# Prompt attention by token parity, in units of 512 columns, two heads issued in alternation

## The chip, the cores and the metric

The kernel runs on one core of a Trainium2 chip. Times are device microseconds of one execution. Five engines work beside each other: TensorE (PE, with its weight loads as PEld), VectorE (DVE), ScalarE (ACT), GpSimd (POOL) and SyncE (SP, which issues most DMAs). TensorE's clock is granted at one of two levels, 1.2 or 2.4 GHz, shown as 0.5 and 1.0 of full speed.

## The reference

One inference step of a two-layer decoder, for a prompt of 256 tokens and 32 sample tokens (8 sequences of 4) together, in float32. Each layer: RMSNorm, one input projection to pool, query, key, value and gate columns, a pooling branch, an attention branch, a merge, and a feed-forward part (dense in layer 0, top 2 of 8 experts in layer 1). What the change touches is the attention of the prompt:

```
ATT_GROUPS = ((128, 1), (512, 4), (2048, 16))     # window, dilation of 3 head groups, 8 heads of 64 each
sc = einsum('bnqhd,bnkhd->bnhqk', qs, kb) * 64 ** -0.5 - slope * distance    # keys at 0 <= distance <= window,
                                                                              # distance a multiple of the dilation
o, lse = softmax(sc) @ v, logsumexp(sc)
y = sum over the 3 groups of o * softmax over the groups of lse
```

For one head number and one query, mixing the three groups by their denominators is one softmax over the keys of all three groups side by side. In the groups with dilation 4 and 16 a query at an even token sees keys at even tokens alone, and one at an odd token keys at odd tokens. The normalised keys and the values of the prompt are outputs too.

## The kernel before

The whole program is written out per engine, each with its own instruction order; PSUM's eight banks are handed out ahead of time by `plan` (one list of jobs per section, in which each name takes the next bank of its pool). `wait_free` waits for a bank, `wait_full` for its data, `wait_read` until it has been read.

A layer's attention part begins with 40 column tiles of the input projection (four pool tiles and n = 0 to 35), each of 24 float32r matmuls over 288 tokens. Queries and keys stand transposed in `qT` and `kT` (dimension on partitions, two heads of 64 per tile). Behind certain column tiles follow the jobs of `AFTER` (line 178). `ROW_TILES` (line 182) puts the jobs "kt" and "vt" there: keys and values of a group are turned to token rows, keys copied by DVE to one of two `k_tok` buffers and stored by POOL's DMAs, values copied by ACT to `v_tok`. DVE waits for the store of two row tiles ago before it overwrites a buffer.

Then comes the prompt attention: 16 units per layer (line 140), one for each pair of heads `j` (0 to 3), tile of 128 queries `qt` and head `e` of the pair. With `qt` = 0 a unit has 3 x 128 score columns, with `qt` = 1 it has 3 x 256. For a unit,

- `scores` (line 889, PE) multiplies 128 queries with the keys, one matmul for each group (float32, two records each in the trace), contracting over the 64 partitions of the head;
- DVE adds the distance table times the slope (line 1652) and takes the maximum (1659), ACT the exponential with its sum (1336), DVE the reciprocal (1662), POOL scales the probabilities in place (2007);
- `turn_probs` (902, PE) turns the probabilities in tiles of 128, ACT copies them to `probsT`;
- `values` (913, PE) multiplies with `v_tok`, into 64 partitions of a bank that both heads share; DVE copies it to `attT`.

The loop at line 1000 issues in step u: scores of unit u, turns of unit u - 2, values of unit u - 3, and from u = 3 on two cache tiles. A cache tile (`cache_step`, 987) belongs to the sample tokens' attention: a 128 x 512 piece of the key cache is turned by four PE instructions and copied by ACT (even tiles) or DVE (odd ones). Four tiles make a chunk of 1 MB, which is then scored by 16 matmuls of 32 query columns (`score_chunk`, 960); one slot of the five-slot ring is free for SP's next DMA as soon as its chunk is turned. `score_new` (949), the scores of the sample's own keys, stands behind tile 2. 32 of the 72 tiles of keys are done within the loop, the others behind it, then the cache's values, the merge and the output projection.

POOL's order before the first `scale`: the stores of all row tiles, then, once the last value tile is read, a memset of 5632 columns for the sample's query tiles, then the scales, with `place_queries` behind each of the first two.

Of the kernel before, what the change touches and what calls it, by code (L numbers as in the profile page):

```python
# [69 lines left out]
def shape_constants():  # L70
# [4 lines left out]
    dist = np.full((PART, G, 2, PART), MASKED)  # L75
    for g in range(G):
        for kind in range(2):
            d = p - f + PART * (1 - kind)
            ok = (d >= 0) & (d <= SPAN[g]) & (d % DIL[g] == 0)
            dist[:, g, kind] = np.where(ok, d, MASKED)  # L80
# [82 lines left out]
FIRST_UNIT = 3  # L163


def unit_tiles(u):
    at = 2 * (u - FIRST_UNIT)
    return [m for m in (at, at + 1) if 0 <= m < NT]


REST = unit_tiles(len(UNITS) + 2)[-1] + 1

# [26 lines left out]
def section_attention():  # L199
# [7 lines left out]
    for u in range(len(UNITS) + 3):  # L207
        if u < len(UNITS):
            js += [(("S", u, n), UPOOL) for n in range(1 + UNITS[u][1])]
        if 2 <= u < len(UNITS) + 2:  # L210
            js += [(("T", u - 2, n), UPOOL) for n in range(1 + UNITS[u - 2][1])]
        if u >= 3 and UNITS[u - 3][2] == 0:
            js.append((("O", UNITS[u - 3][0], UNITS[u - 3][1]), UPOOL))
        js += [(("kT", 0, m), UKPOOL) for m in unit_tiles(u)]
# [107 lines left out]
def build(nc, io):  # L322
# [9 lines left out]
    with ctx:  # L332
# [51 lines left out]
        dist = view(take(G * 2 * 128), G, 2 * 128)  # L384
# [36 lines left out]
        probs = [view(p_at + 768 * i, 768) for i in range(3)]  # L421
        probsT = [view(p_at + 768 * (3 + i), 768) for i in range(2)]
# [121 lines left out]
        p_ready = Tally(sem("probs_ready"), 16)  # L544
# [210 lines left out]
        def _(e):  # L755
# [56 lines left out]
            def attention(L):  # L812
# [33 lines left out]
                def turn_rows(job, tile, a, n, count=4):  # L846

                    S.wait_free(e, job)
                    for i in range(count):
                        turn(S.ps(job)[0:n, 128 * i:128 * (i + 1)], tile(i)[:, a:a + n],  # L850
                             full[S.bank(job)] if i == count - 1 else None)

# [3 lines left out]
                for n in range(36):  # L856
# [3 lines left out]
                    for job in AFTER.get(n, []):  # L860
# [28 lines left out]
                def scores(u):  # L889
                    j, qt, he = UNITS[u]  # L890
                    p = slice(64 * he, 64 * he + 64)
                    w = 128 * (qt + 1)
                    for n in range(1 + qt):
                        S.wait_free(e, ("S", u, n))
                    for g in range(G):
                        job = ("S", u, 1 if qt and g == 2 else 0)
                        last = g == 2 or (qt and g == 1)
                        at = 0 if qt and g == 2 else g * w
                        mm(S.ps(job)[:, at:at + w], qT[p, 4 * g + j, 128 * qt:128 * qt + 128],
                           kT[p, 4 * g + j, 0:w], True, True, full[S.bank(job)] if last else None)  # L900

                def turn_probs(u):
                    j, qt, he = UNITS[u]
                    e.wait_ge(p_ready.sem, p_ready.at(L, u + 1))
                    n = G * (qt + 1)
                    for i in range(n):
                        job = ("T", u, i // 4)
                        if i % 4 == 0:
                            S.wait_free(e, job)
                        turn(S.ps(job)[:, 128 * (i % 4):128 * (i % 4 + 1)], probs[u % 3][:, 128 * i:128 * (i + 1)],  # L910
                             full[S.bank(job)] if i == n - 1 or i % 4 == 3 else None)

                def values(u):
                    j, qt, he = UNITS[u]
                    job = ("O", j, qt)
                    if he == 0:
                        S.wait_free(e, job)
                    for n in range(1 + qt):
                        S.wait_read(e, ("T", u, n))
                    n = G * (qt + 1)  # L920
                    for i in range(n):
                        g, kt = i // (qt + 1), i % (qt + 1)
                        h = 2 * j + he
                        mm(S.ps(job)[64 * he:64 * he + 64, 0:128], v_tok[:, kt, g, 64 * h:64 * h + 64],
                           probsT[u % 2][:, 128 * i:128 * (i + 1)], i == 0, i == n - 1,
                           full[S.bank(job)] if he == 1 and i == n - 1 else None)
# [71 lines left out]
                S.wait_read(e, ("kt", 2, 2))  # L998
                S.wait_read(e, ("vt", 2, 2))
                for u in range(len(UNITS) + 3):  # L1000
                    if u < len(UNITS):
                        scores(u)
                    if 2 <= u < len(UNITS) + 2:
                        turn_probs(u - 2)
                    if u >= 3:
                        values(u - 3)
                    for m in unit_tiles(u):
# [230 lines left out]
        def _(e):  # L1238
# [46 lines left out]
            def attention(L):  # L1285
# [6 lines left out]

                split_high(L, 2)
                for n in range(37):
# [32 lines left out]
                for u in range(len(UNITS) + 3):  # L1327
                    if 2 <= u < len(UNITS) + 2:
                        v = u - 2
                        for n in range(1 + UNITS[v][1]):  # L1330
                            w = min(512, 128 * G * (UNITS[v][1] + 1) - 512 * n)
                            copy(S, ("T", v, n), probsT[v % 2][:, 512 * n:512 * n + w], S.ps(("T", v, n))[:, 0:w])
                    if u < len(UNITS):
                        w = 128 * G * (UNITS[u][1] + 1)
                        e.wait_ge(max_ready.sem, max_ready.at(L, u + 1))
                        e.activation(probs[u % 3][:, 0:w], probs[u % 3][:, 0:w], ACT.Exp, bias=stats[:, u:u + 1],
                                     accum_out=stats[:, 16 + u:17 + u]).then_inc(exp_ready.sem, 1)
                    for m in unit_tiles(u):
                        cache_copy(m)
# [770 lines left out]
```

## Time and profile before

| | |
|---|---|
| median of 3 runs | 2279.5 us (2277.4 to 2279.97) |
| profiled execution | 2273.52 us, span 2271.6 us |
| mean granted clock of TensorE | 0.954 |
| TensorE busy | 2125.1 us (94%) |
| VectorE busy | 1397.4 us (62%) |
| ScalarE busy | 1148.7 us (51%) |
| GpSimd busy | 162.5 us (7%) |
| read from HBM | 542.15 MB, 242 GB/s over the span |

Busy shares are means over stages with different limits, so a stage has to be looked at by itself. Matmuls are pipelined and their ends are modelled: a group of them is shown a little longer than the distance to the next group's start. The prompt attention lies near 185 to 268 us for layer 0 and near 874 to 956 us for layer 1.

### The profile page before, as it was taken

The page shows a single profiled execution, that of the slowest core. Times are in us where ns is not written, and L with a number is a line of the kernel's source. Part 1 is how long each engine was busy: PE and PEld are TensorE (multiplying, and loading weights), DVE is VectorE, ACT ScalarE, POOL GpSimd, SP SyncE. Part 2 cuts the span into 40 slices and gives each one's busy share as a digit, 9 for nine tenths or more (in the row PEclk, how much of TensorE's full clock was granted, in tenths as well). Part 3 has the DMA queues.
Part 4 walks back from the last instruction along what each step waited for, and adds up shares of the span by engine and source line. Part 5 has one row for each costly group of instructions (what it writes and reads, how often), then busy time and mean ns, then how long its engine had stood idle before and what let it go on. Part 6 is the DMA issues. An engine that isn't in the chain of part 4 may idle for free.

```text
span 2271.6 us, 33081 instructions
## 1 busy us (share of the span) xinstructions
PE 2125.1 (94%) x13193; PEld 1801.2 (79%) x13194; DVE 1397.4 (62%) x1338; ACT 1148.7 (51%) x1107; POOL 162.5 (7%) x244
## 2 busy tenths in 40 slices
PE   6998986989999998987988999999999999999998
PEld 6987744989998987753987787887878787887876
DVE  4454422444435444421437888888898888888886
ACT  3443322334433433421325766667676667667674
POOL 0113100102210113200100000000000000000000
PEclk9998987989999998986998999999999999999999
DMA  7442488435544442469427999999999999999994
GB/s 225 155 139 96 131 306 269 154 112 163 166 167 146 159 137 93 149 217 321 149 75 251 352 339 332 352 322 349 331 338 335 343 350 317 356 323 345 335 338 173
DMA packets 292914, 551.19 MB, mean 243 GB/s; under 512 B 10708, under 2 KB 107132, under 8 KB 292658
## 3 DMA queue, kind: packets, MB, share of 16 engines
q1 hardware_dynamic: 288592, 541.53, 68.4%
q0 software_dynamic: 3072, 8.00, 1.0%
q8 instruction: 84, 1.38, 0.2%
q10 hardware_dynamic: 1138, 0.06, 0.0%
q14 instruction: 28, 0.23, 0.0%
HBM read 542.15 MB, written 7.76 MB: 242 GB/s over the span
## 4 chain that ended last, share of the span: by engine, by line
PE 79%; DVE 10%; issue 5%; DMA 3%; ACT 1%; POOL 1%; DVEq 0%; SPq 0%; ACTq 0%; POOLq 0%
PE psum L766 73%; PE psum L774 6%; DVE expert_split L1849 5%; DMA low_part<-in_cache_kv_g 2%; DMA low_part<-in_w_in 1%; DVE low_part L1902 1%; ACT w_split L1261 1%; DVE w_split L1514 1%; POOL high_part L2002 0%; DVE high_part L1525 0%; DVE high_part L1521 0%; DMA high_part<-in_const_a 0%; DVE low_part L1915 0%; DVE hT_split L1855 0%; POOL merged_split L2058 0%
## 5 line engine op out<-in xcount | busy, mean ns | idle before, releaser
L1849 DVE TENSOR_TENSOR expert_split<-low_part,expert_split 128x2048 fp32r<-128x2048 f32 x336 | 764.2, 2288 | 91.2 <-ACT expert_split L1448 91.2
L1448 ACT ACTIVATE expert_split<-low_part 128x2048 fp32r<-128x2048 f32 x336 | 644.1, 1918 | 204.0 <-PE psum L766 202.1
L766 PE MATMUL psum<-expert_split,xe_split 128*128 128x512 f32 x2688 | 638.9, 394 | 11.3 <-DVE expert_split L1849 10.2
L766 PEld LDWEIGHTS psum<-expert_split,xe_split 128*128 128x128 f32 x2688 | 496.9, 188 | 136.4 <-DVE expert_split L1849 27.8
L766 PE MATMUL psum<-xn_split,w_split 128*128 128x288 f32 x3744 | 520.4, 300 | 26.0 <-DVE xn_split L1529 14.4
L766 PEld LDWEIGHTS psum<-xn_split,w_split 128*128 128x128 f32 x3744 | 509.8, 191 | 40.7 <-issue 24.5
L1514 DVE TENSOR_TENSOR w_split<-low_part,w_split 128x2048 fp32r<-128x2048 f32 x105 | 240.9, 2295 | 366.5 <-ACT w_split L1261 366.5
L1261 ACT ACTIVATE w_split<-low_part 128x2048 fp32r<-128x2048 f32 x105 | 200.9, 1913 | 375.1 <-PE psum L766 275.4
L766 PE MATMUL psum<-expert_split,hT_split 128*128 128x512 f32 x1344 | 319.1, 397 | 0.0
L766 PEld LDWEIGHTS psum<-expert_split,hT_split 128*128 128x128 f32 x1344 | 250.8, 188 | 58.7 <-DVE expert_split L1849 2.1
L766 PE MATMUL psum<-low_part 128*128 128x128 f32 (+5 forms) x1198 | 211.8, 449 | 35.5 <-DMA low_part<-in_cache_kv_g 25.1
L766 PEld LDWEIGHTS psum<-low_part 128*128 128x128 f32 (+3 forms) x1198 | 130.5, 173 | 103.2 <-DMA low_part<-in_cache_kv_g 46.4
L774 PE MATMUL psum<-high_part,low_part 128*128 128x128 f32 (+2 forms) x1097 | 159.4, 288 | 23.1 <-DMA high_part<-in_const_a 9.6
L1507 DVE COPY low_part<-psum 128x512 f32<-128x512 f32 (+7 forms) x110 | 64.2, 590 | 173.4 <-PE psum L774 114.4
L774 PEld LDWEIGHTS psum<-high_part,low_part 128*128 128x128 f32 (+2 forms) x1097 | 128.9, 146 | 53.0 <-issue 20.8
L1241 ACT ACTIVATE low_part<-psum 128x512 f32<-128x512 f32 (+2 forms) x144 | 77.1, 557 | 158.1 <-PE psum L774 151.0
L1915 DVE TENSOR_TENSOR low_part<-low_part,psum 128x512 f32<-128x512 f32 x56 | 38.5, 688 | 54.0 <-PE psum L766 54.0
L766 PE MATMUL psum<-hid_split,w_split 128*128 128x288 f32 x528 | 70.1, 294 | 0.0
L766 PEld LDWEIGHTS psum<-hid_split,w_split 128*128 128x128 f32 x528 | 70.0, 188 | 0.0
L766 PE MATMUL psum<-low_part,high_part 128*32 128x128 f32 (+1 forms) x1260 | 59.5, 289 | 8.7 <-POOL high_part L2020 4.9
L766 PE MATMUL psum<-branch_split,w_split 128*128 128x288 f32 x384 | 55.8, 306 | 10.1 <-DVE branch_split L1727 10.1
L766 PE MATMUL psum<-merged_split,w_split 128*128 128x288 f32 x384 | 56.7, 313 | 7.6 <-POOL merged_split L2058 7.6
(134 smaller groups left out, 1065.5 us busy)
## 6 DMA issues: line engine op xcount, KB each, us to landing
low_part<-in_we_gate SPq DMA_DIRECT2D x112, 1024.0 KB, 5.2
low_part<-in_we_up SPq DMA_DIRECT2D x112, 1024.0 KB, 6.4
low_part<-in_we_down SPq DMA_DIRECT2D x112, 1024.0 KB, 6.1
low_part<-in_cache_kv_g SPq DMA_DIRECT2D x72, 1024.0 KB, 5.5
low_part<-in_w_in SPq DMA_DIRECT2D x56, 1024.0 KB, 5.1
low_part<-in_w_dense SPq DMA_DIRECT2D x33, 1024.0 KB, 5.3
low_part<-in_w_out SPq DMA_DIRECT2D x8, 1024.0 KB, 4.9
low_part<-in_w_branch_pool SPq DMA_DIRECT2D x8, 512.0 KB, 5.4
```

What stands on the lines that cost most here:

```text
L766: signal(e.matmul(out, lhsT, rhs, start=start, stop=stop, skip_group_check=mixed), inc)
L774: signal(e.transpose(out, in_, ident[0:in_.shape[0], 0:in_.shape[0]]), inc)
L1241: S.freed(e.activation(out, in_, ACT.Copy), job)
L1261: e.activation(w_split[gw % SRING][:, 0, :], view(slot(c), CH), ACT.Copy).then_inc(hi_ready, 1)
L1448: e.activation(e_split[v % MSRING][:, 0, :], view(slot(v, MRING), CH), ACT.Copy).then_inc(hi_ready, 1)
L1507: S.freed(e.tensor_copy(out, in_), job)
L1514: e.tensor_tensor(s[:, 1, :], view(slot(c), CH), s[:, 0, :].bitcast(F32), ALU.subtract).then_inc(lo_ready, 1)
L1849: e.tensor_tensor(w[:, 1, :], view(slot(v, MRING), CH), w[:, 0, :].bitcast(F32), ALU.subtract)\
L1902: I.freed(e.tensor_tensor(x, x, I.ps(job)[0:n], ALU.add), job)
L1915: I.freed(e.tensor_tensor(m_h[c % 2], m_sig[c % 2], I.ps(("eu", c)), ALU.mult), ("eu", c))
```

## The change

Units are now (j, qt), with `qt` the parity of the query tokens (even or odd), and a unit has 512 score columns: 256 keys of group 0 and the 128 keys of the same parity of groups 1 and 2. The two heads of a unit are issued in alternation, scores and values alike, each with its own PSUM bank for scores and turned probabilities. The order of a step, the order of the scales and the place of the first scores are new. Value rows of groups 1 and 2 lie sorted by parity in `v_tok` (and are stored to every second row of the output), the output of a unit goes to every second token of `attT`.

```diff
-    return [(j, qt, e) for j in range(J) for qt in range(2) for e in range(2)]
+    return [(j, qt) for j in range(J) for qt in range(2)]
+NU = len(UNITS)
+BLOCK_AT, BLOCK_W = (0, 256, 384), (256, 128, 128)
+ACT_SCALED = 2
+def step_tiles(v, part):
+    at = BH * (v - FIRST_STEP) + 2 * part          # FIRST_STEP = 2
+    return [m for m in (at, at + 1) if 0 <= m < NT]
+REST = step_tiles(NU, 1)[-1] + 1
+SCORES_AT = 34
...
+        if n == SCORES_AT:
+            js += [(("S", 0, he), SUMS) for he in range(2)]
+    for v in range(NU + 1):
+        if v + 1 < NU:
+            js += [(("S", v + 1, he), UPOOL) for he in range(2)]
+        js += [(("kT", 0, m), UKPOOL) for m in step_tiles(v, 0)]
+        if v >= 1:
+            js.append((("O", v - 1), UPOOL))
+        js += [(("kT", 0, m), UKPOOL) for m in step_tiles(v, 1)]
+        if v < NU:
+            js += [(("T", v, he), UPOOL) for he in range(2)]
...
-        probs = [view(p_at + 768 * i, 768) for i in range(3)]
+        probs = [view(p_at + 512 * i, 512) for i in range(4)]
...
+        def tile_tokens(row, qt):
+            return row.rearrange("p (a r) -> p r a", r=2)[:, qt, :]
... TensorE
+                def scores(v):
+                    j, qt = UNITS[v]
+                    for he in range(2):
+                        S.wait_free(e, ("S", v, he))
+                    for g in range(G):
+                        at, w = BLOCK_AT[g], BLOCK_W[g]
+                        for he in range(2):
+                            p = slice(64 * he, 64 * he + 64)
+                            keys = kT[p, 4 * g + j, 0:SEQ]
+                            mm(S.ps(("S", v, he))[:, at:at + w], tile_tokens(qT[p, 4 * g + j, 0:SEQ], qt),
+                               tile_tokens(keys, qt) if g else keys, True, True,
+                               full[S.bank(("S", v, he))] if g == G - 1 else None)
-                            turn_rows(job, lambda k: vT[i][:, k, :], *TT[job[2]])
+                            turn_rows(job, lambda k: vT[i][:, k, :], *TT[job[2]], strided=i > 0 and job[2] < 2)
+                    if n == SCORES_AT:
+                        S.wait_read(e, ("bc", 23))
+                        scores(0)
+                def turn_probs(v):         # per head: wait for its scale (p_first or p_ready), four turns
+                def values(v):
+                    for i, (g, kt) in enumerate(((0, 0), (0, 1), (1, qt), (2, qt))):
+                        for he in range(2):
+                            h = 2 * j + he
+                            mm(S.ps(job)[64 * he:64 * he + 64, 0:128], v_tok[:, kt, g, 64 * h:64 * h + 64],
+                               probsT[he][:, 128 * i:128 * (i + 1)], i == 0, i == 3,
+                               full[S.bank(job)] if (he, i) == (1, 3) else None)
-                S.wait_read(e, ("kt", 2, 2))
-                S.wait_read(e, ("vt", 2, 2))
+                for v in range(NU + 1):
+                    if v + 1 < NU:
+                        scores(v + 1)
+                    for m in step_tiles(v, 0):
+                        cache_step(m)
+                    if v == 1:
+                        S.wait_read(e, ("vt", 2, 2))
+                    if v >= 1:
+                        values(v - 1)
+                    for m in step_tiles(v, 1):
+                        cache_step(m)
+                    if v < NU:
+                        turn_probs(v)
... ScalarE (soften: wait for the maximum, Exp of 512 columns; scale: wait for the reciprocal, Copy with scale)
+                        if c == 35:
+                            soften(0)
+                            soften(1)
+                scale(0)
+                scale(1)
+                for v in range(NU + 1):
+                    for he in range(2):
+                        for m in step_tiles(v, he):
+                            cache_copy(m)
+                        if v + 1 < NU:
+                            soften(2 * (v + 1) + he)
+                    if v < NU:
+                        for he in range(2):
+                            copy(S, ("T", v, he), probsT[he], S.ps(("T", v, he)))
+                    if v + 1 < ACT_SCALED:
+                        for he in range(2):
+                            scale(2 * (v + 1) + he)
... VectorE (biased: three scalar_tensor_tensor and the maximum of a unit; inverted: its reciprocal)
+                    if c == SCORES_AT + 1:
+                        inverted(0)
+                        inverted(1)
+                    if c == SCORES_AT:             # behind the row copies of this c
+                        biased(0)
+                        biased(1)
+                for v in range(NU + 1):
+                    for he in range(2):
+                        if v + 1 < NU:
+                            biased(2 * (v + 1) + he)
+                        if he == 1 and v + 1 < NU:
+                            inverted(2 * (v + 1))
+                        for m in step_tiles(v, he):
+                            cache_copy(m)
+                    if v + 1 < NU:
+                        inverted(2 * (v + 1) + 1)
+                    if v >= 1:
+                        j, qt = UNITS[v - 1]
+                        copy(S, ("O", v - 1), tile_tokens(attT[:, j, 0:SEQ], qt), S.ps(("O", v - 1))[:, 0:128])
... GpSimd
+                e.wait_ge(zeroed.sem, zeroed.at(L, 1))
+                for he in range(2):
+                    place_queries(0, he)
+                for u in range(2 * ACT_SCALED, 2 * NU):
+                    scale(u)
```

## Rows read from the trace of the kernel before

**Rows 1.** The page's busy table: busy us, share of the span, instructions.

```profile
PE 2125.1 (94%) x13193; PEld 1801.2 (79%) x13194; DVE 1397.4 (62%) x1338; ACT 1148.7 (51%) x1107; POOL 162.5 (7%) x244
```

**Rows 2.** Windows by stage: stretch, its length, busy per engine, granted clock, DMA share.

```profile
185.00:195.00 10.00, 5.28 (x24) 3.77 (x25) 4.76 (x15) 2.78 (x7) 9.17 (x15) 0.56 0.26 93
206.00:214.00 8.00, 8.00 (x43) 6.78 (x46) 2.00 (x6) 1.97 (x5) 0.58 (x1) 0.57 0.42 133
214.00:250.00 36.00, 36.00 (x361) 28.89 (x364) 20.45 (x53) 16.29 (x37) 5.97 (x8) 1.00 0.35 114
```

**Rows 3.** Chain of waits, 140 to 350 us: start, length, what the chain ran through.

```profile
182.32 2.29 DMA out_kv_prompt<-high_part
...
187.70 4.80 POOL high_part L2002
...
249.80 2.50 PE psum L766 x38
...
322.47 10.87 DMA low_part<-in_cache_kv_g
```

**Rows 4.** TensorE's timeline, one period: start, length, line, operation, count.

```profile
231.84 1.08 PE L766 MATMUL psum<-low_part,high_part 128*32 128x128 f32 x32
232.85 1.56 PE L766 MATMUL psum<-low_part 64*128 64x256 f32 x6
234.34 0.55 PE L774 MATMUL psum<-high_part,low_part 128*128 128x128 f32 x3
234.82 1.52 PE L766 MATMUL psum<-low_part 128*64 128x128 f32 x12
236.27 1.09 PE L774 MATMUL psum<-high_part,low_part 128*128 128x128 f32 x8
...
242.09 0.93 PE L766 MATMUL psum<-low_part 64*128 64x128 f32 x6
242.96 0.88 PE L774 MATMUL psum<-high_part,low_part 128*128 128x128 f32 x6
243.76 0.87 PE L766 MATMUL psum<-low_part 128*64 128x128 f32 x6
...
249.73 1.08 PE L766 MATMUL psum<-low_part,high_part 128*32 128x128 f32 x32
```

**Rows 5.** TensorE's timeline at the stage's start and end.

```profile
185.36 3.40 PE L766 MATMUL psum<-low_part 64*128 64x128 f32 x18 [1.95 <-DVE high_part L1507]
193.12 0.90 PE L774 MATMUL psum<-high_part,low_part 128*128 128x128 f32 x3 [4.36 <-POOL low_part L2007]
...
199.11 1.47 PE L774 MATMUL psum<-high_part,low_part 128*128 128x128 f32 x8
...
203.47 2.76 PE L766 MATMUL psum<-low_part,high_part 128*128 128x32 f32 x24
...
264.73 1.09 PE L774 MATMUL psum<-high_part,low_part 128*128 128x128 f32 x8
...
266.76 1.52 PE L766 MATMUL psum<-low_part 128*64 128x128 f32 x12
```

**Rows 6.** TensorE's timeline: four matmuls on the whole array, four on row strips.

```profile
110.22 0.77 PE L766 MATMUL psum<-high_part,low_part 32*128 32x288 f32 x8
...
142.32 2.10 PE L766 MATMUL psum<-low_part 128*128 128x288 f32 x8
```

**Rows 7.** Groups by line and shape, 185 to 272 us, and ScalarE's, 214 to 259 us.

```profile
L1652 DVE SCALAR_TENSOR_TENSOR low_part<-high_part,psum 128x256 f32<-128x256 f32 x24 | 8.7, 416 | 10.2 <-PE psum L766 10.1
L1659 DVE TENSOR_REDUCE high_part<-low_part 128x1 f32<-128x768 f32 x8 | 7.6, 953 | 0.8
L1652 DVE SCALAR_TENSOR_TENSOR low_part<-high_part,psum 128x128 f32<-128x128 f32 x24 | 5.5, 282 | 4.4 <-PE psum L766 4.2
L1659 DVE TENSOR_REDUCE high_part<-low_part 128x1 f32<-128x384 f32 x8 | 4.4, 553 | 0.3
...
L1336 ACT ACTIVATE low_part<-low_part,high_part 128x768 f32<-128x768 f32 x6 | 5.6, 939 | 4.6 <-DVE high_part L1659 4.6
```

**Rows 8.** VectorE's timeline: the third key row copies of groups 1 and 2.

```profile
180.15 0.68 DVE L1507 COPY high_part<-psum 32x512 f32<-32x512 f32 x1 [2.01 <-DMA out_kv_prompt<-high_part]
...
184.63 0.68 DVE L1507 COPY high_part<-psum 32x512 f32<-32x512 f32 x1 [0.92 <-DMA out_kv_prompt<-high_part]
```

More of the change, by code:

```diff
@@ L74, in shape_constants @@
     band = (np.arange(2 * QUAD)[None, :] == QUAD + p // HD)
[L75 to L80, printed above, removed]
+    dist = np.zeros((PART, 6 * PART))
+    keys = np.arange(SEQ)[None, :]
+    for at, g, d in ((0, 0, 2 * p - keys), (SEQ, 0, 2 * p + 1 - keys), (2 * SEQ, 1, 2 * (p - f)), (2 * SEQ + PART, 2, 2 * (p - f))):
+        ok = (d >= 0) & (d <= SPAN[g]) & (d % DIL[g] == 0)
+        dist[:, at:at + d.shape[1]] = np.where(ok, d, MASKED)
     inv = np.zeros((PART, PG, 16))
@@ L383, in build @@
         band = view(take(2 * QUAD), 2 * QUAD)
-        dist = view(take(G * 2 * 128), G, 2 * 128)
+        dist = view(take(6 * 128), 6 * 128)
         inv_count = view(take(PG * 16), PG, 16)
@@ L885, in attention @@
                             S.wait_read(e, ("zv", 4 * i + 3))
-                            turn_rows(job, lambda k: vT[i][:, k, :], *TT[job[2]])
[L889 to L911, printed above, removed]
@@ new lines, in attention @@
+                    if n == SCORES_AT:
[3 more added lines that the diff above has]
+                    for he in range(2):
+                        job, u = ("T", v, he), 2 * v + he
+                        if v < ACT_SCALED:
+                            e.wait_ge(p_first.sem, p_first.at(L, u + 1))
+                        else:
+                            e.wait_ge(p_ready.sem, p_ready.at(L, u + 1 - 2 * ACT_SCALED))
+                        S.wait_free(e, job)
+                        for i in range(4):
+                            turn(S.ps(job)[:, 128 * i:128 * (i + 1)], probs[u % 4][:, 128 * i:128 * (i + 1)],
+                                 full[S.bank(job)] if i == 3 else None)
@@ L1592, in mean, with biased, inverted @@
                         .then_inc(mean_ready.sem, 1)
+                def biased(u):
+                    v, he = u // 2, u % 2
+                    j, qt = UNITS[v]
+                    job, p = ("S", v, he), probs[u % 4]
+                    S.wait_full(e, job)
+                    for g in range(G):
+                        at, w = BLOCK_AT[g], BLOCK_W[g]
+                        table = SEQ * qt if g == 0 else 2 * SEQ + PART * (g - 1)
+                        r = e.scalar_tensor_tensor(out=p[:, at:at + w], in0=dist[:, table:table + w],
+                                                   scalar=-float(SLOPES[g, 2 * j + he]), in1=S.ps(job)[:, at:at + w],
+                                                   op0=ALU.mult, op1=ALU.add)
+                    S.freed(r, job)
+                    S.wait_read(e, job)
+                    e.tensor_reduce(stats[:, u:u + 1], p, AX.X, ALU.max, negate=True).then_inc(max_ready.sem, 1)
+                def inverted(u):
+                    e.wait_ge(exp_ready.sem, exp_ready.at(L, u + 1))
+                    e.reciprocal(stats[:, 32 + u:33 + u], stats[:, 16 + u:17 + u]).then_inc(rden_ready.sem, 1)
                 rows = 0
@@ new lines, in attention @@
+                for v in range(NU + 1):
+                    for he in range(2):
+                        if v + 1 < NU:
[8 more added lines that the diff above has]
+                        j, qt = UNITS[v - 1]
+                        copy(S, ("O", v - 1), tile_tokens(attT[:, j, 0:SEQ], qt),
+                             S.ps(("O", v - 1))[:, 0:128])
```

110 lines of the change are left out of this document (24 added, 86 removed).

## The prediction, on record before the result

> **What bounds the kernel now.** I read the page's busy table first, then windows by stage, then the chain of waits, then TensorE's timeline through one period of the prompt attention. TensorE is busy for 94% of the span [rows 1], but that average hides stages. The change touches one stage of each layer: from the last column tile of the input projection to the last prompt unit, about 183 to 268 us in layer 0 [rows 5, 8], and the same stretch of layer 1, where shapes and order are the same; I work layer 0 and count it twice.
>
> The stage has two halves. At 185 to 195 TensorE is busy for 5.28 of 10 us at a mean clock of 0.56: a start-up in which it waits. From 214 to 250 it is busy for 36.00 of 36 us at clock 1.00, while VectorE has 20.45 and the DMA share is 0.35 [rows 2]. The chain says the same: a 4.80 us GpSimd memset in the start-up, then matmul groups with no wait between them [rows 3]. So the steady part is paid in TensorE time, and TensorE time saved there is saved on the clock, as long as no other engine is late.
>
> One period (four units, eight cache tiles, two score chunks) runs from 231.84 to 249.73, 17.89 us [rows 4]. Each group's busy time overlaps the next by 0.07 us; less that, scores take 1.49 (two key tiles) and 0.86 (one), turns of probabilities 0.48 and 0.81, values 1.45 and 0.80, a pair of cache tiles 1.02, a chunk 1.01. Two of each unit kind, four tile pairs, two chunks: 2 x 5.89 + 4.08 + 2.02 = 17.88, so the period is accounted for. Two units cost 5.89 us on average.
>
> **The change, part by part.** *Fewer columns.* Two old units of the two kinds (averaged) stream 1152 score columns, 9 turns and 9 value matmuls; a new pair (both heads of one parity) streams 1024, 8 and 8. Eight pairs per layer either way. By the widths above a new pair one after the other would cost: scores 2 x 0.50 + 4 x 0.29 = 2.16, turns 1.04, values 8 x 0.242 = 1.94, together 5.14. That alone saves 0.75 per pair.
>
> *Halves side by side.* The heads alternate instruction by instruction; scores contract over partitions 0-63 and 64-127 into different PSUM banks, values write partitions 0-63 and 64-127. The trace shows no 64-wide pair in alternation, but the 32-wide case: four 288-column matmuls on four row strips take 0.77 us where four on the whole array take 2.10 [rows 6], 2.7 times faster; sixteen 128x128 matmuls on column strips take 1.01, 0.063 each against 0.242 for the 64-wide ones in a row [rows 4]. So strips do overlap. Bounds for a scores pair: 2.16 (no overlap) to 1.08 (full); for values 1.94 to 0.97. I take 1.1 and 1.0, near the full end because both strip rows are. A pair then costs 1.1 + 1.04 + 1.0 = 3.14, saving 2.75.
>
> Against this speaks the Trainium skill, "TensorE: Matmul & The Clock Gate", Part 3: it measured 3.07 for four row tiles, not 4. That agrees with the 2.7 here; if two tiles lost in the same proportion (a factor near 1.5, my estimate from that page), scores plus values would be 2.7 instead of 2.1 and the total gain 10 us smaller, inside my range.
>
> *Strided operands.* Queries, the keys of two groups and sixteen turned value tiles are now read at every second token. No row shows a strided TensorE operand; nearest are the contiguous ones. Below: nothing. Above, if a strided stream took twice as long: 0.58 per pair (two of three score waves) and 16 turns at 0.13, together 6.7 us per layer. I take nothing; the upper end goes into the range. The stores of value rows go to alternate rows of the output, rows as long as before, and only the end of the layer waits for them: nothing.
>
> *The start.* Removed: the memset ahead of the first scale (ScalarE now scales the first four units), and 1.95 us of waiting before the first scores [rows 5]. Added: VectorE does bias and maximum of units 0 and 1 among its last row copies, and waits for ScalarE's exponentials before the copies of group 2. VectorE's third copy for group 1 ends at 180.83 whatever is changed, as it waits for a store [rows 8]. One new unit of 512 columns: 0.42 + 2 x 0.28 + 0.69 for the maximum (between 0.55 at 384 and 0.95 at 768 columns) = 1.67 [rows 7]. Two units end at 184.2, the second exponential (0.8, from 0.94 at 768 columns) at 185.0; two row copies at 0.68 to 186.4; the third needs the first one's store to land (2.29 in the chain, [rows 3], after its issue of 0.5), and ends near 189.2. It frees a PSUM bank that the first turn of probabilities needs, and behind it on VectorE stand the biases of units 2 and 3, which ScalarE waits for. What goes with the memset comes back as this queue. From there TensorE goes at half clock, as in the windows and in a turn of three at 0.90 instead of 0.55 [rows 5]: turn 2.4, scores 2.2, values 2.0, turn 2.4, scores 2.2, and about 1 for copies queued behind two exponentials on ScalarE: first cache tile at 201.4, against 199.11 now [rows 5]. Bounds: 196, if the clock holds, to 206.
>
> *The sum.* From that tile: the step with the new keys' scores 1.02 + 1.0 + 0.5 + 2.6 (its 24 records in rows 5, less overlap) + 0.5 + 1.04 = 6.66; five full steps of 3.14 + 2.04 + 1.01 = 6.19, 30.95; the last step, 2.04 + 1.01 + 1.0 = 4.05; together 41.7. The stretch from 206 to 214 ran at mean clock 0.57 with TensorE busy throughout, behind the new keys' scores [rows 2]; I keep its loss, 8 x 0.43 = 3.4. So prompt and 28 cache tiles are done at 246.5. Before, tile 28 begins at 264.73 with 1.45 of values still to come [rows 5]: 266.2. Gain 19.7 us per layer, 39 in both, 40 rounded.
>
> *Who is late next.* VectorE per step: two units 3.34, two cache copies 1.36, reciprocals and output copy about 0.6: 5.3 of 6.19, and the exponential of the second unit lies beside a cache copy. GpSimd's scales of a step have a whole step of lead. After the stage the cache's keys cost TensorE 3.05 per chunk and the values wait for DMA, up to 10.87 us [rows 3]. The ring's five slots are full throughout at 8.9 us per chunk and stay so at 6.19, since the share was 0.35; four tiles move from the stage to behind it at equal cost. So transfers start earlier with the releases, and I pass the whole gain on.
>
> The profiled execution took 2273.52 us (span 2271.6), 6.0 below the median of 2279.5. Its sum gives 2233.5; against the median, the forecast is **2240 us**.
>
> **Rivals.** *The halves don't overlap* (the change doesn't do what it says). For: no 64-wide alternation in the trace. Against: both strip rows. Price 2.0 per pair, 16 of the 19.7 us: 2272 us.
>
> *VectorE takes over.* The Trainium skill, "TensorEngine Tiling (Array Packing)", PSUM Bottleneck, says that tiling speeds up TensorE but not the evacuation, which may become the limit; no row shows it in this stage, where VectorE is at 57%. Worked from rows: its 5.3 plus exposed waits for the exponential and the next scores; with 2 us of them the step is 7.3 and five to six steps lose 6 us per layer: 2252 us.
>
> *Slower: the clock stays down.* At 206 to 214 the clock was at half for most of the stretch, right behind 24 records of 32 columns, with TensorE shown busy for 8.00 of 8.00 us [rows 2, 5]; the paired halves might be followed by the same. Against: 214 to 250 held 1.00 with 64-wide matmuls, turns and strips. At 1.2 GHz throughout, the 41.7 us cost 38 more per layer, 18 after the gain: 2316 us. It decides from the point where half of the stage's work runs at half clock.
>
> **How the numbers follow.** Forecast 0.76, VectorE 0.10, halves 0.08, clock 0.06. The forecast's own ends: 2222 (start at 196, no loss after the new keys' scores) and 2254 (strided streams twice as long). With the VectorE case the range is 2222 to 2262; it leaves out the slow case and most of the serial one. About 0.2% (4.6 us) is what a measurement can tell from no change. Faster: 0.76 + 0.10 + half of the serial case = 0.90; same 0.04; slower 0.06.
>
> **What would show it.** Right: a step of two units near 6.2 us; scores pairs of 12 records near 1.1 and values of 16 near 1.0; clock 1.00 after the new keys' scores; VectorE idle for some tenths per step before each bias; first cache tile at 198 to 204; the wait for cached values as long as before. Wrong: scores pairs near 2.2 (halves serial), near 1.7 (strides), TensorE waiting for VectorE's bank or ScalarE's copies in steady steps, a clock of 0.5 after 225, or a longer DMA wait that eats the gain.

## The result, and the profile after

The changed kernel takes 2218.91 us (median of 4 runs, 2217.25 to 2222.28) against 2279.38 us: a ratio of 0.9738, 95% interval 0.9721 to 0.9755, 60.5 us less. The forecast was 2240 and its range began at 2222, so the time lies 3.1 us outside it: the direction and the mechanism were right, the size was a third too small.

Two parts of it must be kept apart. The profiled executions took 2273.52 and 2222.28 us, 51.2 apart. The one of before lies 5.9 us below its kernel's median, the one of after 3.4 above its own; that is the other 9.2. So what the two traces can explain is 51.2, where the prediction's sum said 39.

The busy table of the page, then windows of the start, of the stretch with the new keys' scores, and of the steady steps (columns as in [rows 2]):

```profile
PE 2081.0 (94%) x13145; PEld 1774.7 (80%) x13146; DVE 1389.7 (63%) x1338; ACT 1147.4 (52%) x1099; POOL 155.3 (7%) x236
```

```profile
185.00:195.00 10.00, 5.19 (x33) 4.19 (x32) 5.84 (x18) 5.93 (x14) 5.55 (x7) 0.74 0.34 121
200.00:206.00 6.00, 6.00 (x65) 5.54 (x62) 3.58 (x10) 2.83 (x6) 2.33 (x5) 0.99 0.01 3
207.00:239.00 32.00, 32.00 (x466) 27.62 (x464) 21.10 (x59) 18.29 (x39) 6.24 (x9) 1.00 0.58 186
```

TensorE is still 94% busy: 44 us of its work are gone and the span shrank with it [rows 1]. The steady part is busy for 32.00 of 32 us as before [rows 2]. What is new is in the second and third rows: around the new keys' scores and behind them the clock stands at 0.99 and 1.00, where 206 to 214 had 0.57 [rows 2].

TensorE's timeline, one steady step of layer 0 and the last one, for [rows 4] and [rows 5]:

```profile
207.14 1.18 PE L777 MATMUL psum<-low_part 64*128 64x256 f32 x12
208.25 1.09 PE L785 MATMUL psum<-high_part,low_part 128*128 128x128 f32 x8
209.27 1.08 PE L777 MATMUL psum<-low_part,high_part 128*32 128x128 f32 x32
210.28 1.09 PE L777 MATMUL psum<-low_part 128*64 128x128 f32 x16
211.31 1.97 PE L785 MATMUL psum<-high_part,low_part 128*128 128x128 f32 x16
213.20 1.18 PE L777 MATMUL psum<-low_part 64*128 64x256 f32 x12
...
239.11 1.97 PE L785 MATMUL psum<-high_part,low_part 128*128 128x128 f32 x16
```

From one pair of scores to the next it is 6.06 us (forecast 6.19). From each start to the next, the scores of both heads take 1.11 (forecast 1.1), their values 1.03 (1.0). The last row holds tiles 26 to 29, so tile 28 begins near 240.1, where the forecast had 246.5 and the kernel before 266.2.

The start, on TensorE, VectorE and GpSimd, for [rows 5], [rows 8] and [rows 3]:

```profile
187.19 1.18 PE L777 MATMUL psum<-low_part 64*128 64x256 f32 x12 [2.13 <-DVE high_part L1535]
190.41 1.94 PE L785 MATMUL psum<-high_part,low_part 128*128 128x128 f32 x8 [2.05 <-DVE high_part L1535]
...
200.56 1.10 PE L785 MATMUL psum<-high_part,low_part 128*128 128x128 f32 x8
...
203.10 2.76 PE L777 MATMUL psum<-low_part,high_part 128*128 128x32 f32 x24
```

```profile
180.40 0.68 DVE L1535 COPY high_part<-psum 32x512 f32<-32x512 f32 x1 [2.02 <-DMA out_kv_prompt<-high_part]
...
189.59 0.68 DVE L1535 COPY high_part<-psum 32x512 f32<-32x512 f32 x1 [2.55 <-DMA out_kv_prompt<-high_part]
...
214.41 0.82 DVE L1631 SCALAR_TENSOR_TENSOR low_part<-high_part,psum 128x256 f32<-128x256 f32 x3 [0.73 <-PE psum L777]
```

```profile
192.65 4.82 POOL L2043 MEMSET high_part<- 128x5632 f32 x1
```

The GpSimd memset still runs, but no work in the chain waits for it. TensorE's two longest waits now end with VectorE, whose third row copy of group 2 waits 2.55 us for a store. That queue was foreseen, with the copy's end at 189.2 and the first cache tile at 201.4; the copy ended at 190.27 and the tile came at 200.56. In the steady part VectorE idles 0.73 us before a bias (0.66 and 0.67 in the next two steps): it isn't the bound.

The chain behind the stage: the wait for the cached values is about as long as before, 11.35 against 10.87 us [rows 3]. The column tiles behind layer 0's attention then begin 25.3 us earlier, so of the 26.1 gained up to tile 28 nearly all is passed on. The wait in the chain, then these column tiles, before and after:

```profile
296.25 11.35 DMA low_part<-in_cache_kv_g
```

```profile
367.55 12.68 PE L766 MATMUL psum<-xn_split,w_split 128*128 128x288 f32 x83 [5.34 <-DVE w_split L1514]
```

```profile
342.28 15.08 PE L777 MATMUL psum<-xn_split,w_split 128*128 128x288 f32 x96 [5.33 <-DVE w_split L1542]
```

A ruler for the experiments: from the new keys' scores of the first half to those of the second, which spans all units but the first ones. It was 73.96 us in layer 0 and 72.36 in layer 1, and is 48.28 and 48.26. These 25.7 and 24.1 make 49.8 of the 51.2 us. The rest is a balance: behind the ruler of layer 1 the kernel before loses another 4.0 us (97.98 against 93.98 to the next column tiles), and the remaining stretches give back 2.6.

### The profile page after: what moved, and what is told of

It reads as the page before. It is cut to its first block, busy times and chain, and to the rows that moved or that the text cites. A ratio compares the mean times of both kernels' runs of the same rounds, so it can differ in the third digit from the quotient of the medians.

```text
span 2220.5 us, 32905 instructions
## 1 busy us (share of the span) xinstructions
PE 2081.0 (94%) x13145; PEld 1774.7 (80%) x13146; DVE 1389.7 (63%) x1338; ACT 1147.4 (52%) x1099; POOL 155.3 (7%) x236
## 4 chain that ended last, share of the span: by engine, by line
PE 79%; DVE 10%; issue 5%; DMA 3%; ACT 2%; POOL 1%; DVEq 0%; SPq 0%; ACTq 0%; POOLq 0%
PE psum L777 74%; DVE expert_split L1890 5%; PE psum L785 5%; DMA low_part<-in_w_in 1%; DMA low_part<-in_cache_kv_g 1%; DVE low_part L1943 1%; ACT w_split L1276 1%; DVE w_split L1542 1%; DMA out_kv_prompt<-high_part 0%; DVE high_part L1553 0%; DVE high_part L1549 0%; DMA high_part<-in_const_a 0%; DVE hT_split L1896 0%; DVE low_part L1956 0%; POOL merged_split L2096 0%
## 5 line engine op out<-in xcount | busy, mean ns | idle before, releaser
L777 PE MATMUL psum<-low_part 128*128 128x128 f32 (+7 forms) x1166 | 166.0, 448 | 36.8 <-DMA low_part<-in_cache_kv_g 23.8
L777 PEld LDWEIGHTS psum<-low_part 128*128 128x128 f32 (+4 forms) x1166 | 99.0, 175 | 95.7 <-issue 41.5
L785 PE MATMUL psum<-high_part,low_part 128*128 128x128 f32 (+2 forms) x1081 | 149.2, 285 | 14.9 <-DMA high_part<-in_const_a 9.7
L1256 ACT ACTIVATE low_part<-psum 128x512 f32<-128x512 f32 (+1 forms) x128 | 72.3, 593 | 105.1 <-PE psum L785 98.3
```

The source lines that it names most:

```text
L777: signal(e.matmul(out, lhsT, rhs, start=start, stop=stop, skip_group_check=mixed), inc)
L785: signal(e.transpose(out, in_, ident[0:in_.shape[0], 0:in_.shape[0]]), inc)
L1256: S.freed(e.activation(out, in_, ACT.Copy), job)
```

## The experiments

**Both kernels again, and two cheap suspicions.** First both kernels, unchanged.

> The kernel before, unchanged, for a second trace. Theory A (the half-clock stretch behind the new keys' scores belongs to the old order of the stage): TensorE's clock is at 0.5 for some 7 us near 206 us in layer 0 and some 3 to 7 us near 896 us in layer 1 again, and tile 28 of layer 0 begins near 264.7 us again. Rival B (where the clock falls is chance from execution to execution): the stretches lie elsewhere or are missing, and the stage's end moves by 2 us or more. Theory C (6 us of the miss is that the profiled execution was shorter than the median): this trace's span is nearer to 2278 than to 2271.6, and the difference lies in stretches at half clock outside the prompt attention. Ratio to the kernel before 1.000.

> The changed kernel, unchanged, for a second trace and a second timing. Theory A: no half clock behind the new keys' scores, tile 28 of layer 0 begins near 240 us, both layers gain 26 to 27 us between the end of the last column tile and the end of the prompt's values. Rival B: a half-clock stretch appears behind the new keys' scores in one layer at least, and the stage is 2 to 4 us longer there. Time 2216 to 2222 us, ratio near 0.974.

Measured: 2277.95 (ratio 0.9994, 0.9981 to 1.0006) and 2215.95 us (0.9721, 0.9689 to 0.9753). The ruler gives 72.41 and 72.42 us in the one, 48.26 and 48.28 in the other.

*Contiguous operands:* TensorE reads halves of the sequence where the change reads every second token; the parity is left out of scores and values.

```diff
+        def half_tokens(row, qt):
+            return row[:, 128 * qt:128 * qt + 128]
-   mm(S.ps(("S", v, he))[:, at:at + w], tile_tokens(qT[p, 4 * g + j, 0:SEQ], qt),
-      tile_tokens(keys, qt) if g else keys, True, True,
+   mm(S.ps(("S", v, he))[:, at:at + w], half_tokens(qT[p, 4 * g + j, 0:SEQ], qt),
+      half_tokens(keys, qt) if g else keys, True, True,
...  (the turned value tiles the same way)
```

> The changed kernel with TensorE's strided operands replaced by contiguous halves of the same size (queries, keys of two groups, turned value tiles); parity is left out of the scores and values by it, so the outputs of the prompt are other numbers. Theory 1 (a stride of two costs TensorE nothing): same time within 0.2%, scores pair 1.11 us. Rival 2 (strided streams are slower): scores pairs 0.1 to 0.5 us shorter, 2 to 10 us in all.

Measured: 2215.85 us (0.9717, 0.9686 to 0.9748), the changed kernel's time. The stride costs next to nothing: the ruler gives 48.15 us in both layers, 0.1 less. The 2254 us end of the forecast falls away. The Trainium skill, "SBUF — State Buffer", Specifications (TRN2), asks for at least two hits in each 16-byte line for full bandwidth, which every second 4-byte token gives; this run agrees.

*Heads one after the other,* in scores and in values, everything else as changed.

```diff
-                    for g in range(G):
-                        at, w = BLOCK_AT[g], BLOCK_W[g]
-                        for he in range(2):
-                            p = slice(64 * he, 64 * he + 64)
+                    for he in range(2):
+                        p = slice(64 * he, 64 * he + 64)
+                        for g in range(G):
+                            at, w = BLOCK_AT[g], BLOCK_W[g]
```

> The changed kernel with the alternation alone undone: all scores of one head, then all of the other, values likewise. Theory 1 (halves overlap, and that is the larger part of the gain): a scores pair takes 2.1 instead of 1.11 us, values 1.9 instead of 1.02, a full step 8.0 instead of 6.06; 8 pairs in 2 layers cost 16 x 1.9 = 30 us, 2250 us. Rival 2 (the gain comes from fewer columns, the earlier start and the clock): less than 8 us slower, below 2227 us. Where VectorE limits the step already, the loss would be smaller than TensorE's own: under 20 us.

The values likewise. Measured: 2229.54 us (0.9776, 0.9742 to 0.9811), 13.6 above the changed kernel's 2215.95; I had expected 30. TensorE's timeline shows why:

```profile
218.99 1.72 PE L777 MATMUL psum<-low_part 64*128 64x256 f32 x12
220.64 1.09 PE L785 MATMUL psum<-high_part,low_part 128*128 128x128 f32 x8
221.66 1.08 PE L777 MATMUL psum<-low_part,high_part 128*32 128x128 f32 x32
222.67 1.58 PE L777 MATMUL psum<-low_part 128*64 128x128 f32 x16
224.18 1.97 PE L785 MATMUL psum<-high_part,low_part 128*128 128x128 f32 x16
226.08 1.25 PE L777 MATMUL psum<-low_part 64*128 64x256 f32 x8
```

A pair of scores takes 1.65 us, not 2.16, and values 1.51, not 1.94; the step is 7.09. Either two heads in a row already overlap, or my price for one head was too high. The next run decides.

**Heads apart.** The serial version, with a cache tile between the two heads, so that each head's instructions form a group of their own.

```diff
-                    if v + 1 < NU:
-                        scores(v + 1)
-                    for m in step_tiles(v, 0):
-                        cache_step(m)
+                    for he in range(2):
+                        if v + 1 < NU:
+                            scores(v + 1, (he,))
+                        for m in step_tiles(v, 0)[he:he + 1]:
+                            cache_step(m)
...  (values and step_tiles(v, 1) the same way)
```

> The serial version (no alternation of heads) with a cache tile between the two heads' scores and between the two heads' values, so that the same columns are issued in four more groups per step. Theory (an issued group carries about 0.2 us beside its columns, which is why the old units were dear and merging them paid): the steady step goes from 7.09 to 7.9 us, six steps in each of two layers make 9 to 10 us, 2239. Rival (only the columns count): step 7.1, 2229 to 2231.

Measured: 2246.12 us (0.9863, 0.9848 to 0.9878), some 29 above the changed kernel (30.2 above 2215.95, 28.3 above 2217.82).

```profile
209.44 1.17 PE L777 MATMUL psum<-low_part 64*128 64x256 f32 x6
210.54 0.66 PE L785 MATMUL psum<-high_part,low_part 128*128 128x128 f32 x4
211.12 1.17 PE L777 MATMUL psum<-low_part 64*128 64x256 f32 x6
212.23 0.66 PE L785 MATMUL psum<-high_part,low_part 128*128 128x128 f32 x4
...
213.82 1.09 PE L777 MATMUL psum<-low_part 128*64 128x128 f32 x8
214.84 0.66 PE L785 MATMUL psum<-high_part,low_part 128*128 128x128 f32 x4
...
217.91 1.17 PE L777 MATMUL psum<-low_part 64*128 64x256 f32 x6
```

One head's scores alone (6 records) take 1.10 us; the two heads in alternation (12 records) take 1.11. The second head is free. One head's 512 columns are priced by [rows 4] at 1.07: 768 columns took 1.49 and 384 took 0.86, so 0.63 per 384 and 0.23 per group. (By the values of [rows 4], 1.45 for six matmuls and 0.80 for three, it is 0.15 per group.) So my price was right for heads apart (2.20 measured, 2.16 forecast), and the plain serial order isn't the case without overlap: it takes 1.65, where two heads' columns alone (2 x 0.84) and one entry of 0.23 would make 1.91. About half of what alternation saves (0.55 of 1.09) is already had; by the same price 0.23 of it is the second group's entry and 0.3 is overlap. The step here is 8.47; of the 1.38 over the serial one 0.55 is scores, 0.53 values (twice 1.02 against 1.51) and 0.3 the split tiles. My theory of 0.2 per group gave 0.8 for four more groups and is too small: the other 0.6 is, by that price, overlap lost.

The ruler now divides the 25.7 us of layer 0. 3.2 are the half clock behind the new keys' scores: in the last experiment below, old units without it need 70.80. From there to heads apart (61.34) it is 9.5, of which 5.9 because the same start now gets more done before the ruler begins: four pairs' scores instead of two and a half, two pairs' turns instead of one and a half, two pairs' values instead of one (1.5 x 2.20 + 0.5 x 1.02 + 2.04); the other 3.6 are fewer columns, less what this version's split tiles cost (about 0.3 per step, in up to six steps). Heads in a row (53.37) take off 8.0, in which the split tiles go again, alternation (48.28) 5.1. Each of these figures is from one profile.

**A gap that the profile doesn't explain.** In layer 1 the kernel before has a gap ahead of a key chunk in which TensorE waits for nothing that the profile shows: 1.56 us in the first profile, 2.38 in the second, and 1.83 in its version with a third row buffer (the last run below). None of the ten profiles with the new units has it. The chain of the second:

```profile
1003.12 1.08 PE psum L766 x32
1004.20 2.38 issue
1006.58 1.11 PE psum L774 x8
```

Behind it the last key chunk with the first cached values takes 12.24 and 13.64 us, where eight of the ten profiles with the new units have 7.40 (the first one has 10.75). From there to the first `branch_split` matmuls behind the attention it is 81.3 and 83.1 us, against 75.5 to 79.8 with the new units. My theory D: the gap depends on where instructions stand in TensorE's program, so part of the gain is luck of layout. Each kernel got extra waits, for something long done, at the head of TensorE's program, meant to run while it waits for its first load anyway (I counted two to an instruction; no trace lists them).

```diff
+            for _ in range(180):          # 154 in the kernel after
+                e.wait_ge(ones_set, 3)
             e.wait_ge(small_loaded, 64)
```

> The kernel before with 90 more instructions at the head of TensorE's program: waits that are long satisfied, in the 9.6 us in which TensorE waits for its first loads anyway. Theory D (the gap of 1.56 us and 2.38 us in layer 1, in which TensorE waits for nothing that the profile shows, belongs to the place of the instructions in TensorE's program): the gap leaves the last key chunks of layer 1, the first values of the cache's 64 matmuls take 7.4 us there instead of 12 to 14, values-to-dense in layer 1 is 76 to 77 us instead of 81 to 83, and the time is 5 to 7 us below the kernel before, near 2273. Rival (the gap belongs to the work done there, or to the time since the start): it stays where it is, and the time is 2279 within 2 us.

> The kernel after with 77 more such waits at the head of TensorE's program, as many instructions as the change took out of it, so that everything from the cached keys of layer 1 on stands at the same place in the program as in the kernel before. Theory D: the gap of 1.5 to 2.4 us appears in front of the last key chunk of layer 1, values-to-dense there goes from 77 to 81 to 83 us, and the time is about 5 us above the kernel after: 2221. Rival (the change itself removed the gap): no gap, 2216 within 2 us.

Measured: 2279.13 us (1.0, 0.9989 to 1.0011) and 2217.82 (0.9736, 0.9723 to 0.975). In the one profile of the padded kernel before the gap is gone; the stretch behind it still took 79.6 us, and the time stayed. In the kernel after no gap came. But the waits were not free, as this row of the padded kernel before shows:

```profile
12.29 4.05 PE L774 MATMUL psum<-high_part,low_part 128*128 128x128 f32 x25 [12.29 <-issue]
```

TensorE's first matmul had begun at 9.58, and the long run of columns now begins at 31.19 instead of 28.66 (in the kernel after 29.90 instead of 28.81). So an unchanged time can hide some 2.5 us that the gap's going gave back; the 5 to 7 us of theory D didn't come. As a price for more than a small part of the gain theory D falls.

**The start, part by part.** *First scores back behind the columns* (scores, bias and exponential of units 0 and 1 moved together):

```diff
-                    if n == SCORES_AT:
-                        S.wait_read(e, ("bc", 23))
-                        scores(0)
+                S.wait_read(e, ("bc", 23))
+                scores(0)
                 for v in range(NU + 1):
...  (ScalarE and VectorE the same way)
```

> The kernel after without its early first scores: scores, bias, maximum and exponential of units 0 and 1 come behind the last columns and row copies, as in the kernel before. Theory (the row copies that wait for their stores set the start, and the early units only change places with them on VectorE): the first turn of probabilities moves by less than 1.5 us, and the time is 2216 to 2220. Rival (the early scores take a whole preparation of two units, about 3 us, out of the start): 5 to 7 us over the kernel after, 2221 to 2223.

Measured: 2212.45 us (0.9701, 0.9686 to 0.9716): both expectations too high. The early scores gain nothing; if anything they cost some us. The first turn of probabilities comes at 191.11 instead of 190.41, but the row copies they had pushed back end earlier, and GpSimd's memset behind them begins at 189.10 instead of 192.65. (This profiled execution, 2217.56 us, lies 5 above its kernel's median, so it can't show where the lower time comes from.)

```profile
186.03 0.68 DVE L1532 COPY high_part<-psum 32x512 f32<-32x512 f32 x1 [0.94 <-DMA out_kv_prompt<-high_part]
```

*All scales on GpSimd,* as in the kernel before:

```diff
-ACT_SCALED = 2
+ACT_SCALED = 0
```

> The kernel after with all scales on GpSimd behind its memset, as in the kernel before; the four first scales stand ahead of the placing of the queries. GpSimd's memset ends at 197.5 in the kernel after, ScalarE's first scales at 188.3. Theory (giving the first scales to ScalarE is what keeps the memset out of the chain): the first turn of probabilities goes from 190.4 to about 198.5, of which the clock and the queues behind may give back some: 5 to 8 us per layer, 2227 to 2232. Rival (the row copies and the exponentials hold the start anyway): under 2 us per layer, 2216 to 2220.

Measured: 2231.77 us (0.9796, 0.9781 to 0.981), about 13 to 16 above the changed kernel, as the theory said. TensorE waits for the memset's engine:

```profile
197.79 1.97 PE L785 MATMUL psum<-high_part,low_part 128*128 128x128 f32 x8 [9.72 <-POOL low_part L2045]
```

*A third buffer for key rows,* in a free place of the probabilities' space, with the first inversions behind the row copies:

```diff
-        k_tok = view(k_tok_at, 2, 512)
+        k_tok = [view(a, 512) for a in (k_tok_at, k_tok_at + 512, p_at + 3072)]
...
-   if rows >= 2:
-       e.wait_ge(k_stored[rows % 2], 16 * (L * (len(K_STORES) // 2) + rows // 2))
+   if rows >= 3:
+       e.wait_ge(k_stored[rows % 3], 16 * (L * K_TURNS[rows % 3] + rows // 3))
...  (K_TURNS counts each buffer's stores; inverted(0) and inverted(1) move behind the row copies)
```

> The kernel after with a third buffer for key rows on their way to the store, and VectorE copies the rows of group 2 before it inverts the first sums. Theory (the start is bound by the row copies that wait for stores: 2.0 us at 180.4 and 2.55 us at 189.6): the bias of unit 2 begins at 187 instead of 190.2, the first cache tile is reached 2 to 3.5 us earlier (197 to 198.5), 4 to 7 us in two layers: 2211. Rival (ScalarE's exponentials and copies, 182.4 to 188.3, and the half clock set the start): first cache tile within 1 us of 200.6, 2216 within 2 us.

Measured: 2204.59 us (0.9676, 0.9663 to 0.9689), 11 to 14 below the changed kernel, twice what I expected: the best version of all. Two things move here, the buffer and the place of the first inversions; no run parts them.

```profile
187.65 0.82 DVE L1632 SCALAR_TENSOR_TENSOR low_part<-high_part,psum 128x256 f32<-128x256 f32 x3 [0.35 <-PE psum L778]
```

```profile
185.00:195.00 10.00, 7.40 (x74) 6.02 (x74) 7.62 (x24) 9.54 (x21) 8.68 (x12) 1.00 0.34 121
```

The bias of unit 2 begins at 187.65 instead of 190.19, TensorE is busy for 7.40 instead of 5.19 of the 10 us, and the clock is 1.00 there instead of 0.74: the waits had cost twice there, in themselves and in the clock behind them. From the long run of columns to the new keys' scores it is 119.2 and 120.5 us in the two layers, against 121.3 to 125.5 in four profiles of the changed kernel and its harmless variants.

*The same, with the first exponential ahead of ScalarE's last column copy:*

```diff
+                        if c == 35:
+                            soften(0)
                         copy(S, ("zv", v), vT[v // 4][:, v % 4, :], S.ps(("zv", v))[:, 0:T])
                         if c == 35:
-                            soften(0)
                             soften(1)
```

> The version with three row buffers, with the first exponential ahead of ScalarE's last value-column copy, so that the table load of 1.28 us lies beside TensorE's last column. Theory (TensorE's wait of 1.58 us at 189.2 in that version ends with ScalarE's scales, and those stand behind the table load): first turn of probabilities at 188.0, 1 us per layer, 2202 to 2203. Rival (the copies of the turned values between them hold the scales): within 1 us of the three-buffer version, 2204.6.

Measured: 2205.75 us (0.9678, 0.9665 to 0.9691), no change. TensorE's timeline:

```profile
186.77 1.27 PE L786 MATMUL psum<-high_part,low_part 128*128 128x128 f32 x8 [0.23 <-ACT low_part L1316]
187.97 1.18 PE L778 MATMUL psum<-low_part 64*128 64x256 f32 x12
191.52 1.09 PE L778 MATMUL psum<-low_part 128*64 128x128 f32 x16 [2.37 <-ACT low_part L1257]
```

The wait before the first turn shrank from 1.58 to 0.23 us, the next one, before the first values, grew from 1.02 to 2.37: moved, not removed.

*The third buffer in the kernel before* (the same edit, with a wait for the last store ahead of the copies that reuse the place):

> The kernel before with the third row buffer alone. Theory (the queue of row copies sits in both kernels; in the kernel before, GpSimd's memset stands behind the stores of these rows, so 0.99 and 0.92 us of waiting on VectorE delay it): the memset begins 1.5 to 2 us earlier, 3 to 4 us in all, 2274 to 2276. Rival (there the wait lies beside other work, and only the change brought it into the chain): within 1.5 us of the kernel before.

Measured: 2273.64 us (0.9977, 0.9966 to 0.9987), 5.1 less. GpSimd's memset begins at 186.50 instead of 187.69. In this profile the half clock behind layer 0's new keys' scores is missing too, the 3.2 us of the ruler. So this queue cost time in both kernels; the 11 to 14 us of the changed one hold the moved inversions as well.

## Why the prediction was right or wrong, point by point

- *What bounds the stage, and who isn't late next: right.* TensorE has no wait in the steady steps; VectorE keeps 0.7 us to spare, so that rival has nothing. Nearly the whole gain went through the wait for DMA (25.3 of 26.1 us in layer 0).
- *Halves side by side: right,* at the full end, 1.11 and 1.03. (The strip row's 2.7 was of busy times; from start to start it is 0.69 against 1.73, so 2.5.) The Trainium skill, "TensorE: Matmul & The Clock Gate", Part 3, has 3.07 for four row tiles and no figure for two; my estimate of 1.5 from it was too low: 2.20 to 1.11 is a factor of 2.0, and the measurement decides. What I had wrong is what the rival meant: without alternation the heads cost 13.6 us, not 32, since two heads in a row already overlap in part and pay one entry; only heads apart cost some 29 us.
- *Strided operands: right,* next to nothing (0.1 us per layer).
- *The start: right in its mechanism.* What goes with the memset came back as VectorE's queue of row copies, whose last one ended at 190.27 against my "ends near 189.2". That the first cache tile still came 0.84 us earlier than forecast is luck: the pieces from there, mostly at half clock, took 10.3 us instead of 12.2 (a turn 1.9, not 2.4). The early scores, which I counted as a help, are none; what pays is ScalarE's share of the scales.
- *The sum: here it failed.* Tile 28 of layer 0 begins 6.4 us earlier than forecast. "I keep its loss, 8 x 0.43 = 3.4" is the largest term, and it measured nothing: none of the ten profiles with the new units shows the half clock behind the new keys' scores, in either layer. I counted five steps with scores, one too many: 1.1. Steps of 6.06 instead of 6.19 give 0.65, the start 0.84. That is 6.0 of the 6.4, and 12 us when layer 0 is counted twice, as the prediction did.
- *The base: this failed too, by 9 us.* I moved the sum from the profiled execution to the median by 6.0 us, as if the changed kernel's executions stood to theirs alike. Its profiled one lies 3.4 on the other side. The low end of the range, 2222, rests on the same conversion; 9 us lower it would have taken in the measured time.

Why the clock stays up is not settled. In three profiles of the kernel before it was down behind the new keys' scores of layer 0 (granted clock of 209 to 214: 0.54, 0.66, 0.56); with the third row buffer alone, and the old units unchanged, it was 1.00 there, while in layer 1 it still fell (0.50 at 893 to 896). The window of 209 to 214, in the kernel before and with the third buffer:

```profile
209.00:214.00 5.00, 5.00 (x28) 4.17 (x30) 0.57 (x2) 1.97 (x5) 0.58 (x1) 0.54 0.58 193
```

```profile
209.00:214.00 5.00, 5.00 (x60) 3.85 (x58) 2.80 (x6) 1.20 (x3) 0.00 (x0) 1.00 0.32 120
```

So the columns of the new keys' scores alone don't bring it down, as I took it, nor does a long wait ahead of them: after the 9.72 us wait above, the clock was back up before those scores. I have no run that sets it at will. Nor did I find what the unexplained gap is.

## What to carry to other kernels

Price a group of matmuls as its columns plus an entry (0.15 to 0.23 us here), and put matmuls that use different halves of the array next to each other: about half of the saving comes from not parting them, the other half from alternating them. Where a wait at a start is taken away, look at the queue behind it at once: here undoing that queue (a third row buffer, inversions behind the copies) gave 11 to 14 us, about what taking the first scales off GpSimd had given (13 to 16). And a stretch at half clock is a term of its own, which may go with the wait ahead of it; give it a range, not its old value.

## What the runs showed of the hardware

- Two 64-row halves: 6 records of one head take 1.10 us, 12 of two heads in alternation 1.11, 12 one head after the other 1.65. Two 64-column halves: 1.02 (8 records), 1.03 and 1.51 us (16).
- TensorE operands read at every second fp32 element cost next to nothing: 2215.85 us without the stride against 2215.95.
- A gap of 1.56 to 2.38 us in which TensorE waits for nothing visible, in three profiles of the old units, was missing in the one with 180 more waits at the program's head, a millisecond earlier.
- The same program's executions differ by up to 15 us (2273.70 to 2288.82 in 13 of the kernel before): a single profile can't measure less.
